# Gather steps of 32 tokens with four slots each, all V sums on TensorE, x rows repeated by ScalarE

## The reference

```python
e = experts.reshape(n, -1)                 # 8 heads x 16 = 128 experts per token, of 16384
g = jax.nn.softmax(best, axis=-1)
ue = jnp.take(u, e, axis=0)
h = jax.nn.gelu(jnp.einsum('nkd,nd->nk', ue, xt), approximate=False)
ve = jnp.take(v, e, axis=0)
f = jnp.einsum('nk,nkd->nd', (g * h), ve)  # x = x + f
```

## Time and profile before

| | |
|---|---|
| runs (three) | 3978.09, 3979.85, 3986.93 us; median 3979.85 |
| span of the profiled execution | 3979.7 us |
| busy: TensorE, VectorE, ScalarE, GpSimd | 3171.9 (80%), 2654.8 (67%), 1461.1 (37%), 1531.1 us (38%) |
| moved | 1340.72 MB, of which 1108.54 MB gathers; mean 337 GB/s |
| first dot, last dot | 650.5 us, 3969.2 us |

### The profile page before, as it was taken

The page is one execution under the profiler, slowest core; times in us unless marked ns, Lnnn a source line. Parts: engine busy times, 40 slices in busy tenths (PEclk is TensorE's granted clock), DMA queues, the critical chain, the costliest instruction groups (busy, mean ns, idle before and its releaser), DMA issues.

```text
span 3979.7 us, 46667 instructions
## 1 busy us (share of the span) xinstructions
PE 3171.9 (80%) x14264; PEld 1436.6 (36%) x14264; DVE 2654.8 (67%) x6242; ACT 1461.1 (37%) x4359; POOL 1531.1 (38%) x1405
## 2 busy tenths in 40 slices
PE   6999988788987999797788887876879666666655
PEld 3555545333433554353333333544425211111110
DVE  3443016988888964778677876885568864556664
ACT  2222001355654244223456564233323333333332
POOL 2111002355655433434445554442344443444333
PEclk9999999889998999898899988888889776776676
DMA  4223336799999999988789999999999999999998
GB/s 157 97 92 102 101 122 257 266 354 340 408 365 387 416 417 392 403 342 342 293 333 375 377 352 397 416 362 368 400 420 404 370 420 420 420 420 419 411 394 346
DMA packets 257065, 1340.72 MB, mean 337 GB/s; under 512 B 31472, under 2 KB 70128, under 8 KB 121392
## 3 DMA queue, kind: packets, MB, share of 16 engines
q0 software_dynamic: 152400, 1108.54, 69.3%
q1 hardware_dynamic: 79344, 204.15, 14.0%
q10 hardware_dynamic: 25072, 25.04, 1.8%
HBM read 1310.49 MB, written 27.15 MB: 336 GB/s over the span
## 4 chain that ended last, share of the span: by engine, by line
PE 42%; DMA 24%; DVE 17%; ACT 6%; issue 4%; DVEq 3%; SPq 2%; ACTq 1%; POOL 1%; POOLq 0%
DMA ringx<-in_peer_uv,tl_idx 12%; DMA mix<-in_peer_uv,tl_idx 11%; PE tl_ps L939 9%; PE tl_ps L991 8%; PE tl_ps L775 6%; PE tl_ps L974 4%; PE tl_ps L923 3%; PE tl_ps L950 3%; PE tl_ps L840 3%; DVE ringx L1610 3%; DVE mix L1610 3%; PE tl_ps L753 2%; DVE tl_xa L1621 2%; PE tl_ps L809 2%; SPq L611 1%
## 5 line engine op out<-in xcount | busy, mean ns | idle before, releaser
L701 POOL DMA_INDIRECT mix<-in_peer_uv,tl_idx x528 | 626.0, 1186 | 782.9 <-PE tl_ps L991 432.8
L701 POOL DMA_INDIRECT ringx<-in_peer_uv,tl_idx x528 | 612.7, 1160 | 731.7 <-PE tl_ps L991 450.8
L1610 DVE CUSTOM_DVE_ANT_0 mix<-mix,tl_xb 128x1024 f32<-128x1024 f32 x528 | 640.9, 1222 | 296.2 <-DMA mix<-in_peer_uv,tl_idx 288.3
L1610 DVE CUSTOM_DVE_ANT_0 ringx<-ringx,tl_xb 128x1024 f32<-128x1024 f32 x528 | 640.7, 1222 | 277.8 <-DMA ringx<-in_peer_uv,tl_idx 270.1
L991 PE MATMUL tl_ps<-ringx,tl_dg 64*64 64x512 f32 x3352 | 569.7, 764 | 298.8 <-ACT tl_dg L1235 298.3
L991 PE MATMUL tl_ps<-mix,tl_dg 64*64 64x512 f32 x3288 | 566.9, 775 | 280.3 <-ACT tl_dg L1235 256.7
L1224 ACT ACTIVATE tl_hg<-tl_hd 128x1 f32<-128x1 f32 x1056 | 213.3, 202 | 1560.9 <-DVE tl_hd L1610 1545.8
L939 PE MATMUL tl_ps<-tl_xr,low 128*128 128x384 f32 (+1 forms) x1280 | 401.9, 470 | 32.2 <-DMA low<-in_wall 27.7
L1228 ACT ACTIVATE tl_hw<-tl_hg,tl_gw 128x1 f32<-128x1 f32 x1056 | 310.9, 294 | 76.1 <-issue 4.6
L991 PEld LDWEIGHTS tl_ps<-ringx,tl_dg 64*64 64x64 f32 x3352 | 105.6, 155 | 639.4 <-ACT tl_dg L1235 566.8
L991 PEld LDWEIGHTS tl_ps<-mix,tl_dg 64*64 64x64 f32 x3288 | 104.9, 157 | 617.8 <-ACT tl_dg L1235 512.6
(11 more groups left out here) (193 smaller groups left out, 4002.1 us busy)
## 6 DMA issues: line engine op xcount, KB each, us to landing
low<-in_wall SPq DMA_DIRECT2D x240, 512.0 KB, 7.9
low<-in_watt SPq DMA_DIRECT2D x60, 512.0 KB, 9.0
mix<-in_peer_uv,tl_idx POOLq DMA_INDIRECT x528, 13.6
ringx<-in_peer_uv,tl_idx POOLq DMA_INDIRECT x528, 13.6
ringx<-in_watt SPq DMA_DIRECT2D x12, 512.0 KB, 5.9
tl_u<-in_x_prompt SPq DMA_DIRECT2D x8, 512.0 KB, 11.8
x_rows<-tl_u SPq DMA_DIRECT2D x8, 512.0 KB, 8.1
xs_rows<-tl_u SPq DMA_DIRECT2D x8, 512.0 KB, 7.5
```

Of the source, the lines that this page charges most:

```text
L701: nc.gpsimd.indirect_dma_start(out=ring[q % RING].rearrange("p a d -> p (a d)"), out_offset=None, in_=A["peer_uv"], in_offset=bass.Indirec ...
L1610: nc.vector.tensor_tensor_reduce(out=ring[q % RING][:, 0, :], in0=ring[q % RING][:, 0, :], in1=xb[:, t % 2, :], scale=1.0, scalar=0.0, op0 ...
```

## The change

A step now handles 32 tokens with four slots each: partition quadrant b holds slot b of the step's four. A tile of 128 tokens is four passes of 32 steps (tile 0: passes of 8 steps, so that it can begin when only two heads are routed). `place(q)` gives tile, quarter g of its tokens, and step j within the quarter.
- `weigh` does all 1056 steps on TensorE, with a diagonal of 128 rows and 32 columns (four slots fold onto 32 tokens): four pieces of 128x32 with 256 columns, each to its own quadrant of the output.
- `by_dve`, `add_row`, `add_start`, the copy and the turn at a tile's end, and the sample's copies and merging are gone. VectorE adds a finished pass's sum to xa (128x256) three steps after the pass (`add_sums`). Sums alternate between two banks.
- The tables must be laid out by quadrant: `by_quadrants` makes 16 small copies for idx and 16 for gw in each unit of routing (4 and 4 for the sample).
- The rows xb of a pass are 32 rows, loaded once, and repeated to the three other quadrants by ScalarE (three copies per pass, 45 passes). Load and copies are issued three to five steps apart.
- The residual is loaded and the result stored in four DMAs each with pieces of 1 KB.
- The four last units of routing begin at other steps, because both of a tile's units are now needed within its first 16 steps.
ATT, PLAN and the ring are unchanged.

```diff
-SHARED = ((0,170,1,6),(170,300,3,4),(336,520,1,6),(520,680,2,3))
-           (388, 4), (450, 5), (514, 5), (560, 5), (713, 3), (745, 4), (850, 4), (900, 4), (950, 4), (985, 4))
+           (388, 4), (450, 5), (514, 5), (560, 5), (713, 3), (745, 4), (800, 4), (850, 4), (910, 4), (960, 4))
...
+def place(q):
     t, k = divmod(q, SLOTS)
+    if t == 0:
+        return t, k // 8 % QUAD, k // 32 * 8 + k % 8
+    return t, k // TOKS, k % TOKS
...
             def gather(q):
                 if q >= RING:
-                    if npe(q + 1 - RING) > npe(q - RING):
-                        pool.wait_ge(s["used_pe"], npe(q + 1 - RING))
-                    else:
-                        pool.wait_ge(s["used_dve"], ndve(q + 1 - RING))
+                    pool.wait_ge(s["used_pe"], q + 1 - RING)
...
             def weigh(q):
+                t, g, j = place(q)
+                pe.wait_ge(s["dg_done"], q + 1)
+                if q == 0:
                     pe.wait_ge(s["n_cp"], 6)
-                for b, h in quarters:
-                    rows = half_of(b)
-                    last = nc.tensor.matmul(ps[half_of(h), b, :], dg[rows, npe(q) % DIAGS, :],
-                                            ring[q % RING][rows, 1, h * 512:(h + 1) * 512], start=k == 0,
-                                            stop=t == NT and k == DEC - 1, skip_group_check=True)
+                elif j == (0 if t else 24) and QUAD * t + g > 1:
+                    pe.wait_ge(s["summed"], QUAD * t + g - 1)
+                for b in range(QUAD):
+                    last = nc.tensor.matmul(sums(g, b), dg[:, q % DIAGS, :], ring[q % RING][:, 1, b * COLS:(b + 1) * COLS],
+                                            start=j == 0 and g < 2, stop=j == TOKS - 1, skip_group_check=True)
                 last.then_inc(s["used_pe"], 1)
...
+            def load_row(p):
+                first, t, g = PASSES[p]
                 act.wait_ge(s["xs_out"], 48 * (t // 3 + 1))
+                act.dma_start(xb[quadrant(0), p % 2, :], A["xs"][t * P + g * TOKS:t * P + (g + 1) * TOKS, :]).then_inc(s["row_in"], 16)
+            def repeat_row(p, b):
+                act.wait_ge(s["row_in"], 16 * (p + 1))
+                nc.scalar.copy(xb[quadrant(b), p % 2, :], xb[quadrant(0), p % 2, :]).then_inc(s["rows_done"], 1)
...
+                slot(q)
+                p = PASS_AT.get(q, 0) + 1
+                if q in PASS_AT and p < len(PASSES):
+                    load_row(p)
+                p = PASS_AT.get(q // 8 * 8, 0) + 1
+                if q // 8 * 8 in PASS_AT and p < len(PASSES) and 3 <= q % 8 < 6:
+                    repeat_row(p, q % 8 - 2)
+                if k == 5 and t:
+                    store_y(t - 1)
+                if k == 10 and t:
                     load_x1(t)
...
+            def by_quadrants(dst, src, t, h0, nh):
+                n = QUAD * nh
+                for g in range(1 if t == NT else QUAD):
+                    first = h0 // 2 * 32 + g * 8 if t == 0 else g * TOKS + QUAD * h0
+                    for b in range(QUAD):
+                        nc.vector.tensor_copy(dst[quadrant(b), t % 2, first:first + n], src[quadrant(g), b * n:(b + 1) * n])
...
+            def add_sums(q):
+                t, g, j = place(q)
+                dve.wait_ge(s["used_pe"], q + 1)
+                if g == 0:
+                    dve.wait_ge(s["xa_in"], 64 * (t + 1))
+                nc.vector.tensor_tensor(xa[:, g, :], ps[:, g % 2, g // 2 * COLS:(g // 2 + 1) * COLS], xa[:, g, :],
+                                        ALU.add).then_inc(s["summed"], 1)
...
             for q in range(LAST):
-                if q == NT * SLOTS:
-                    for p in range(4):
-                        quad = slice(p * DEC, (p + 1) * DEC)
-                        nc.vector.tensor_copy(idx[quad, 1, 0:DEC], idx[quad, 0, quad])
-                        nc.vector.tensor_copy(gw[quad, 1, 0:DEC], gw[quad, 0, quad])
                 dot(q)
                 for step in steps:
                     advance(step, q)
-                if q >= 2 and by_dve(q - 2):
-                    add_row(q - 2)
+                if q >= EVICT and place(q - EVICT)[2] == TOKS - 1:
+                    add_sums(q - EVICT)
+            add_sums(LAST - 1)
```

More of the change, by code:

```diff
@@ L196, in _, with pass_length, sums_done @@
                 last.then_inc(s["tr_done"], 1)
-def by_dve(q):
+def place(q):
     t, k = divmod(q, SLOTS)
-    if not (4 if t == 0 else 14) <= k < SLOTS - 4:
-        return False
-    return any(first <= q < end and q * share % whole < share for first, end, share, whole in SHARED)
-def ndve(q):
-    return sum(by_dve(i) for i in range(max(q, 0)))
-def npe(q):
-    return max(q, 0) - ndve(q)
+    if t == 0:
+        return t, k // 8 % QUAD, k // 32 * 8 + k % 8
+    return t, k // TOKS, k % TOKS
+def pass_length(t):
+    return 8 if t == 0 else TOKS
+PASSES = [(k, 0, k // 8 % QUAD) for k in range(0, SLOTS, 8)] + [(k, k // SLOTS, k % SLOTS // TOKS) for k in range(SLOTS, NT * SLOTS + TOKS, TOKS)]
+PASS_AT = {first: p for p, (first, t, g) in enumerate(PASSES)}
+def sums_done(t, g):
+    return QUAD * t + g + 1
 def plan(rb):
@@ L580, in _ @@
             attend(0)
-            for rb in range(PASSES):
+            for rb in range(NB):
                 tiles = BLOCKS[rb][2]
@@ L1010, in _ @@
                     advance(step, q)
[L1011 to L1023 removed]
+                if q >= LAG:
+                    weigh(q - LAG)
+            for q in range(LAST - LAG, LAST):
+                weigh(q)
         @block.scalar
@@ L1628, in _ @@
             nc.vector.drain().then_inc(s["setup"], 1)
-            steps = [started(norms())] + [started(part(rb)) for rb in range(PASSES) for part in (attend, middle)] + [started(routing())]
+            steps = [started(norms())] + [started(part(rb)) for rb in range(NB) for part in (attend, middle)] + [started(routing())]
             for q in range(START, 0):
```

198 lines of the change are left out of this document (70 added, 128 removed).

## The result

The changed kernel is slower: 4033.26 us median (4029.62 to 4053.16, four runs) against 3979.18 of before, ratio 1.0144 with a 95% interval of 1.0117 to 1.0171. A second series of the same program gave 4023.87 us, ratio 1.0120 (1.0100 to 1.0140). The forecast was 3972 us, the range 3925 to 4020.

The account below looks back on a forecast made before the run. It took VectorE to bound A, TensorE and DMA nearly tied B, DMA the last stretch, neither C. Start +2, A -5, B +24, C -19, D 0, turn, end and pieces -10: -8 on 3979.7, 3972 us; range 3925 to 4020.

Parts of the forecast that it names:

- A: Steps 0 to 172, end of block 0's routing and block 1's attention, VectorE busiest: forecast -5 us.
- C: Block 2's attention, steps 333 to 520, neither TensorE nor DMA full: forecast -19 us, the largest saving.
- Rival 3: The four 128-row pieces of a sum overlap incompletely: about 4130 us in pairs (chance 0.03), some 4020 in part (0.05).
- B: Block 1's dense projections, steps 172 to 333, TensorE and DMA nearly tied as limits: forecast +24 us, ends +12 and +36.
- The turn to the sample: Around step 1024, where no gather runs ahead while VectorE copies the index table: forecast -7.6 us.
- D: Block 2's projections, steps 520 to 704: DMA covers TensorE's added work, forecast 0, ends -8 and +20 us.
- Wrong if: Eight records over 1 us; a unit's copies over 6; ScalarE's copies waiting over 30 for row loads; B not longer.
- Right: Profile signs: short sums, B longer with TensorE busier, C 15 to 25 us shorter, step 768 onward shorter, 0.13 us copies.
- Gathers alone: The last stretch, where DMA is full: +1.5 us for the further DMA issues a tile in 1 KB pieces.
- Rival 1: Slower: TensorE limits the dense stages, D's cover runs out, A gives 0: +33, 4012 us, chance 0.23.
- Rival 4: ScalarE's waits for row loads hold up the attention: +30, 4002 us, chance 0.06.
- rival 2: Faster: relief of both engines counts whole in C, more in A: -58 at most, 3943 with half, chance 0.19.

Follow-up runs that it names:

- no_copies: The changed kernel without ScalarE's row copies and with one table copy in place of VectorE's 16 small ones (results wrong): 3964.72 us, ratio 0.9964.
- rows_once: The changed kernel without ScalarE's copies of the rows and without the waits for them (three quadrants keep older rows): 3993.69 us, ratio 1.0033.
- rows_later: The changed kernel with ScalarE's three row copies of a pass two steps later, at steps 5 to 7: 4025.13 us, ratio 1.0119.
- no_copies_wide: As no_copies, but each of the four 128x32 pieces of a sum streams 512 columns instead of 256 (sums wrong): 4031.05 us, ratio 1.0123.
- Before_all_pe: The kernel before with all V sums on TensorE as 64x64 pieces, no step on VectorE: 4037.41 us, ratio 1.0153.
- before_small_pieces: The kernel before with the residual loaded and the result stored in 1 KB pieces: 3981.76 us, ratio 1.0015.
- rows_by_dma: The changed kernel with three more row loads a pass in place of ScalarE's copies: 4067.21 us, ratio 1.0227.

## Why the prediction was wrong, step by step

**The step that failed.** The forecast priced what is taken away and what is added in the attention stages by the share of each in the chain of waits of the kernel before. The V sums and VectorE's adds were credited with -30 us in A and -27 in C (their new adds and diagonals included); no_copies against before shows -18 and -11. The small table copies were charged +20 us and cost 30; ScalarE's copies were charged +15 and cost 36.

**What held.** The saving on one sum: 0.43 us forecast, 0.45 measured (1.11 to 0.66), with four pieces side by side; the 0.75 for a sum holds 0.09 more than the distance between dense records, and its 0.16 for the end of a record stands in no row. Rival 3 is out. The 2.38x for three pieces that the Trainium skill states (TensorE: Matmul & The Clock Gate, Packing small matmuls) would have made a sum 0.11 us longer than forecast, by the prediction's estimate. The trace doesn't agree: 0.64 us for the eight records, where 0.65 was forecast without that loss. B: +26.5 against +24, with TensorE at 96.5% and the DMA share at 0.97, at the edge of what the test of the forecast asked (above 97%, below 0.97). The turn to the sample, -6.7 against -7.6 with the gap at step 1024 gone, and the end, -3.3 against -3.5. D: -4.6, within its ends and within the scatter. These are the steps worked out from a limit (an engine at 95% or more, a gap between two dots). None of the four signs under "Wrong if" came up, so they didn't guard the steps that failed. Of the signs under "Right", three missed: C is not shorter, the stretch from step 768 to the end is 3 us shorter instead of 10, and a small copy takes 0.18 us instead of 0.13; the sums' share of C's chain fell even further than forecast, to 5.3%.

**VectorE's table copies, the first wrong size.** I had 0.134 us a copy and half of A's on the path: +2 and +15, and +3 in C. Rows_once against no_copies, which differ by these copies alone, gives 4.4 us to the first gather, 13.7 in steps 0 to 32, 8 in steps 32 to 172 and 7 in C: about 30 us in all by median as by span. Both factors failed. A copy takes 0.18 us, since these copies don't overlap as the pairs of the earlier trace rows do. And the share that is paid differs by stage: in steps 0 to 32, where VectorE is busy 132 of 147 us, 80 copies are busy 13.9 us and all of it is paid; in steps 32 to 172 112 copies are busy 19.9 us and four tenths are paid; in C 128 copies are busy 23.6 us and about three tenths. A's 21.6 us lie inside the ends of 8 and 28 that the forecast gave them.

**ScalarE's copies, the second.** I gave them +7, +3 and +5, and nothing in D. Rows_once against the changed kernel gives 36 us in the profiles and 30 to 40 in the medians: 17 us for the 42 copies in steps 32 to 172 (44 us busy), 8 us for the 18 in C (19 us), 6.5 for the 15 in D. That is four tenths of the copies' time, where I took an eighth in A, its share in the chain of the kernel before. That share was the wrong measure. By the order in the code each copy stands ahead of the next attention piece of ScalarE that VectorE or TensorE waits for; that this is how it costs is argued, no run moves the copies behind such a piece. The chain of the changed kernel has ScalarE's exponentials (L1021, 5.2% and 4.1%), gates and the copies themselves in it where VectorE had been:

```profile
by line: issue 8.1%; DMA tl_xb<-xs_rows 7.7%; ACT tl_u L1021 5.2%; DVE ringx L1600 4.8%; DVE mix L1600 4.8%; ACT L1021 4.1%; ACTq L1191 3.7%; ACT L1190 3.5%; PE tl_ps L763 3.4%; ACT tl_hw L1194 3.3%; PE tl_ps L797 3.0%; ACT tl_xb L1229 3.0%
```

(The chain by line, 801.6 to 1272.3 us.) Its 7.7% of row loads points at the wait, but rows_later shows that two more steps for the load change nothing.

**Narrow sums in the attention, the third and, with the adds, the largest.** -9 in A and -23 in C rested on the share that the sums had in the chain. No_copies against no_copies_wide prices the narrowness directly: -12 in A, +5 in C (no more than the scatter), -56 in B. In C no gain shows at all. The time that a step of the chain has is not the time that its removal gives: with the sums halved, TensorE waits 34 us longer for ScalarE's diagonals in C. The kernels before and after say it too: ahead of the sums of C TensorE is idle for 95 us in the kernel before (162 sums) and 124 in the changed one (187). And 34 of the 77 us that the sums of C save went into slower dense work at the lower clock.

**The adds on VectorE.** I credited -18 -6 in A and -6 in C for L1621. Before_all_pe gives -9 in A and -11 in C with full-width sums in their place, and -13 in D, where I had argued that DMA hides all. A's term was too large; C's and D's can't be told from the forecast by more than the scatter, though three profiles without the adds all lie below the two with them in D.

**Gathers alone.** +7 us in steps 768 to 1023 against +1.5. It is not the 1 KB pieces (before_small_pieces), not ScalarE's copies (rows_once, 658.5), not the small tables (no_copies, 657.8), nor the narrow sums (no_copies_wide, 657.3). All of these runs of the changed kernel still have the 32-row loads, the earlier units of routing and the adds per pass. At 0.85 us each (rows_by_dma) eight loads are 6.8 us, where the two loads of 512 KB that they replace are 2.5 us at 414 GB/s: an estimate of +4.3. But the loads lie evenly over the stretch, and 6.0 of the 7.0 us lie in steps 768 to 896 (331.1 us against 325.1), so they explain half of it at most and the rest stays open.

**The sum of the errors**, from before, no_copies, rows_once and the first profile of the changed kernel: ScalarE's copies +21 (36 for 15), the tables +10 (30 for 20), the sums and the adds in A and C +27 (-30 for -57), gathers alone +5, B +2, D -8 before the copies, the rest 0: 57 us between forecast and span. The three large ones go the same way: savings and added costs were both credited at their share of the chain of before, and where engines take turns in a strict order an addition cost more than that share and a removal gave less. Rival 1 put the loss on TensorE in B and D; D's cover did not run out, and its A ("the copies eat all that the adds leave") was the right direction, but 0 where +25 came with the start. Rival 4 had the right engine and the wrong mechanism. The result lies 13 us outside the range: ScalarE's copies had no ends of their own, and the range did not allow for errors that all go one way because they rest on one rule. A slip in the working: rival 2 with half of its extra gain is 3947, not 3943.

## What to carry to other kernels

Work added to an engine of a hand-ordered pipeline can cost far more than that engine's share of the chain says. Here an eighth was forecast and four tenths were paid for ScalarE's copies in the attention stages; small copies on VectorE cost three to four tenths of their time there, and all of it where VectorE was busy 90%. A cheaper form of an operation pays where its engine is the limit (here -56 us in one dense stage) and can pay little or nothing where engines take turns (here -12 us in one attention stage, none in the other), so apply it, or undo a sharing between engines, stage by stage: taking VectorE's share of the sums away everywhere but in the dense stage gave 0.7%, while the whole change lost 1.2 to 1.4%. And give a forecast signs that test the steps with the least ground: here the four signs of being wrong tested the others.
